# Wider weight transfers in a mixture-of-experts block, and a different hand-over between the engines in its attention and router

## What is computed

```python
proj = rms_norm(x, w) @ w_in                                   # dq, dk, dv, lq, lk, lv
o_diff = rms_norm((softmax(s1) - lam * softmax(s2)) @ dv, subln_w) * (1 - lam_init)
o_dil = (exp(s) * mult / sum(exp(s) * mult)) @ lv              # mult: how many of 3 dilations hold the pair
x1 = x + concat(o_diff, o_dil) @ w_out
h = rms_norm(x1, ffn_norm_w)
logits = h @ router_w + router_b                               # top 4 of 32, gates = softmax of the 4
for e in range(32):                                            # rows of the tokens that chose e
    gu = h[rows] @ w_gate_up[e] + b_gate_up[e]                 # 1024 x 2048: 8 MiB
    y[rows] += gate * ((up + 1) * gate_act @ w_down[e] + b_down[e])   # 1024 x 1024: 4 MiB
out = rms_norm(x1 + y, final_norm_w)
```

## Time and profile before

| | us |
|---|---|
| median of 3 executions (1070.84 to 1072.6) | 1071.29 |
| the profiled execution, its time | 1070.58 |
| its span, first to last instruction | 1068.8 |
| PE busy | 1017.1 (95%) |
| DVE busy | 228.8 (21%) |
| ACT busy | 119.1 (11%) |
| POOL busy | 9.4 (1%) |
| DMA, mean over the span | 397 GB/s |

### The profile page before, as it was taken

One profiled execution on the slowest core, in us unless ns is written; L12 is line 12 of the kernel. 1 busy time (PEld: TensorE's weight loads), 2 busy tenths in 40 slices (PEclk: granted clock), 3 DMA queues, 4 the chain that ended last, 5 costly groups with the idle time before them and its releaser, 6 DMA issues.

```text
span 1068.8 us, 12195 instructions
## 1 busy us (share of the span) xinstructions
PE 1017.1 (95%) x4977; PEld 436.6 (41%) x4977; DVE 228.8 (21%) x511; ACT 119.1 (11%) x287; POOL 9.4 (1%) x23
## 2 busy tenths in 40 slices
PE   9999999999999999999999989898998989898996
PEld 8686544434343434343433324242433333242422
DVE  4476443111111111111111101121211111111111
ACT  1133420000000000000000000000000000000001
POOL 1000000000000000000000000000000000000000
PEclk9999999999999999999999999999999999999999
DMA  9936569999999999999999999999999999999996
GB/s 327 389 129 241 187 248 394 426 428 429 426 429 427 425 430 426 427 429 426 427 430 426 429 430 426 429 430 426 429 429 426 430 429 426 430 428 427 430 423 261
DMA packets 37261, 423.90 MB, mean 397 GB/s; under 512 B 6176, under 2 KB 6192, under 8 KB 12048
## 3 DMA queue, kind: packets, MB, share of 16 engines
q1 hardware_dynamic: 35184, 422.80, 94.2%
q10 hardware_dynamic: 2048, 0.67, 0.2%
HBM read 422.41 MB, written 1.05 MB: 396 GB/s over the span
## 4 chain that ended last, share of the span: by engine, by line
PE 58%; DMA 32%; DVE 6%; SPq 2%; issue 1%; ACT 1%; POOL 0%; DVEq 0%
DMA gu_ring<-in_w_gate_up_dram 32%; PE psum L927 21%; PE psum L977 15%; PE psum L889 5%; PE psum L658 5%; PE psum L633 3%; PE psum L663 2%; PE psum L763 2%; DVE mixed L1386 1%; DVE mixed L1382 1%; DVE mixed L1384 1%; SPq L268 1%; PE psum L705 0%; PE psum L913 0%; ACT mixed L573 0%
## 5 line engine op out<-in xcount | busy, mean ns | idle before, releaser
L927 PE MATMUL psum<-gu_ring,mixed 128*64 128x512 f32 x2048 | 453.4, 595 | 33.9 <-DMA gu_ring<-in_w_gate_up_dram 33.9
L927 PEld LDWEIGHTS psum<-gu_ring,mixed 128*64 128x64 f32 x2048 | 140.9, 137 | 324.4 <-issue 252.7
L977 PE MATMUL psum<-dn_ring,mixed 128*64 128x512 f32 x928 | 206.2, 596 | 3.2 <-ACT mixed L573 2.6
L977 PEld LDWEIGHTS psum<-dn_ring,mixed 128*64 128x64 f32 x928 | 64.9, 137 | 127.5 <-issue 121.9
L1382 DVE TENSOR_SCALAR mixed<-psum 128x512 f32<-128x512 f32 x32 | 22.1, 692 | 425.7 <-PE psum L927 425.7
L1339 DVE TENSOR_TENSOR mixed<-posm,iota 128x256 f32<-128x256 f32 x47 | 20.0, 425 | 243.3 <-PE psum L633 242.9
L591 ACT ACTIVATE mixed<-psum 128x512 f32<-128x512 f32 x30 | 17.9, 597 | 447.9 <-PE psum L927 447.9
L908 PE MATMUL psum<-mixed 64*128 64x512 f32 x256 | 63.6, 615 | 0.7 <-ACT mixed L577 0.7
L889 PE MATMUL psum<-mixed,xres 128*128 128x128 f32 x480 | 59.0, 282 | 0.0
L658 PE MATMUL psum<-gu_ring 128*128 128x256 f32 x256 | 57.5, 382 | 1.1 <-ACT gu_ring L472 1.1
L889 PEld LDWEIGHTS psum<-mixed,xres 128*128 128x128 f32 x480 | 57.9, 197 | 0.0
(11 more groups left out here) (152 smaller groups left out, 386.4 us busy)
## 6 DMA issues: line engine op xcount, KB each, us to landing
gu_ring<-in_w_gate_up_dram SPq DMA_DIRECT2D x123, 2048.0 KB, 28.0
dn_ring<-in_w_down_dram SPq DMA_DIRECT2D x56, 2048.0 KB, 20.1
mixed<-in_w_down_dram SPq DMA_DIRECT2D x6, 2048.0 KB, 13.2
gu_ring<-in_w_in_dram SPq DMA_DIRECT2D x11, 1024.0 KB, 16.1
gu_ring<-in_w_gate_up_dram SPq DMA_DIRECT2D x8, 1024.0 KB, 9.0
dn_ring<-in_w_out_dram SPq DMA_DIRECT2D x4, 1024.0 KB, 9.4
dn_ring<-in_w_down_dram SPq DMA_DIRECT2D x3, 1024.0 KB, 22.4
gu_ring<-in_w_gate_up_dram SPq DMA_DIRECT2D x4, 512.0 KB, 20.9
```

The costliest lines, as they stand in the source:

```text
L927: last = mm(bank[b0 + b][CAP * c:CAP * (c + 1), :], xg[:, k, CAP * half:CAP * (half + 1)], gu_ring[:, 8 * half + k, w0:w0 + 512], start=Fa ...
L977: last = mm(bank[4][CAP * c:CAP * (c + 1), :], actT[:, a0:a0 + CAP], dn_slot[slot][:, k // 2 % 2, w0:w0 + 512], start=False, stop=(k == KT ...
```

## The change

1. **Packets of 32 KB.** Gate/up weights of experts 4 to 31 are laid out with j=4: one chunk then brings each partition four rows, 32 KB side by side. For experts 6 to 29, and the first half of expert 30, a DMA moves such a chunk of 4 MiB (`load_wide`) when two of the former chunks are used; experts 4, 5, the rest of 30 and 31 come in 16 KB (or smaller) parts of those 32 KB. PE waits once in four values of k (`gu_wide`).
2. **x1 turned in place.** To fit j=4 the columns of x1 are rearranged in place before pair 1: ACT copies 512 columns to a PSUM bank, DVE writes them back in the other order, four times, while PE runs `gate_up(1, 0)`; PE waits for the last (`x1_turned`) ahead of pair 1. The gather then reads x1 without a step. The factors of the norm come in a second small load (`ffn_4`).
3. **Dilated heads.** The values are now the stationary operand: `pv_pair` takes two heads, which stand side by side in the array, and gives the result already turned. `pv`, `keep_pv` and `turn_mix` are gone for dilated heads. The division by the sum moves from ACT to POOL (`norm_probs`, two `tensor_scalar` of 256 and 128 columns a head), ahead of the turn. On DVE `dil_probs(g)` stands before `negated_scores(g + 1)` instead of behind it.
4. **Router.** `first_sel` becomes two `tensor_scalar` of 128x64 (compare, then multiply) from `slot0` and `iota_1`; the step L1292 goes behind the first gather; `first_sel(0)` moves ahead of `choose_experts(1)`; the negation for the exponent (L1279) goes behind `chosen_ready`.
5. **Early load.** The second half of w_down of expert 0 comes in two DMAs of 1 MiB; the first is issued when the output projection has used 9 pieces, the second at `x1_done` as before.

```diff
+            def load_wide(e, half, q):
+                r = GUN * half + 4 * q
+                sp.dma_start(gu_ring[:, r:r + 4, :].rearrange("p (e j) c -> p e (j c)", e=1),
+                             gu_v4[:, bass.ds(e, 1), q, :]).then_inc(gu_wide[2 * half + q], 16)
...
                 else:
                     sp.wait_ge(scores_done, 2 * NH)
-                    sp.wait_ge(pv_done, 2 * NH)
+                    sp.wait_ge(pv_done, NH)
+                    sp.wait_ge(mixT_done, NH)
...
             sp.wait_ge(w_out_used, 8)
             load_dn(0, 0, 0)
+            sp.wait_ge(w_out_used, 9)
+            sp.dma_start(dn_ring[:, 2, :], dn_v[:, 0, 1, 0:WS]).then_inc(dn_in[1], 16)
             sp.wait_ge(x1_done, 2 * TT)
-            load_dn(0, 1, 1)
+            sp.dma_start(dn_ring[:, 3, :], dn_v[:, 0, 1, WS:2 * WS]).then_inc(dn_in[1], 16)
...
+            def wide(e, q):
+                sp.wait_ge(gu_used, GUN * (e // 2 - 1) + (4 * (e % 2) + 2 * q + 2) + EXTRA)
+                load_wide(e, e % 2, q)
...
+            def norm_probs(g):
+                pool.wait_ge(sums_ready, g - NH + 1)
+                z = 40 + 2 * (g % 2)
+                for c, w, a in ((0, T, 1), (T, P, 0)):
+                    pr = probs[g % 2][:, c:c + w]
+                    last = nc.gpsimd.tensor_scalar(pr, pr, st[:, z + a:z + a + 1], None, ALU.mult)
+                last.then_inc(probs_ready, 1)
...
+            for i in range(2 * TT):
+                if i:
+                    act.wait_ge(x1_turned, i)
+                nc.scalar.activation(bank[7][:, :], xres[:, i // 2, 512 * (i % 2):512 * (i % 2 + 1)], ACT.Copy)\
+                    .then_inc(x1_copied, 1)
...
+            def pv_pair(g):
+
+                if g == NH:
+                    pe.wait_ge(v_ready, 2)
+                    pe.wait_ge(pv_read, NH)
+                pe.wait_ge(probsT_ready, g + 2)
+                pe.wait_ge(mixT_ready, g // 2)
+                for b in range(2):
+                    for m in range(2):
+                        last = mm(bank[7][HD * m:HD * (m + 1), P + P * b:P + T], vS[:, b, HD * (g + m):HD * (g + m + 1)],
+                                  probsT[m][:, T * b:T + P * b], start=(b == 0), stop=(b == 1), skip_group_check=True)
+                last.then_inc(mixT_done, 1)
...
-                if g + 1 < 2 * NH:
+                if g < NH:
                     negated_scores(g + 1)
-                if g < NH:
                     diff_probs(g)
                 else:
                     dil_probs(g)
+                    if g + 1 < 2 * NH:
+                        negated_scores(g + 1)
...
             def first_sel(a):
-                link(V.tensor_tensor(sel[:, a, :, :], posm[:, a, 2:4].unsqueeze(2).broadcast_to([P, 2, CAP]),
-                                     iota[:, :].unsqueeze(1).broadcast_to([P, 2, CAP]), ALU.is_equal))
-                flat = sel[:, a, :, :].rearrange("p e n -> p (e n)")
-                return V.tensor_scalar(flat, flat, st[:, 2 + a:3 + a], None, ALU.mult)
+                for e in range(2):
+                    last = V.tensor_scalar(sel[:, a, e, :], iota_1, slot0[:, a, e:e + 1], st[:, 2 + a:3 + a],
+                                           ALU.is_equal, ALU.mult)
+                return last
...
+            for i in range(2 * TT):
+                dve.wait_ge(x1_copied, i + 1)
+                V.tensor_copy(xres[:, i // 2, 512 * (i % 2):512 * (i % 2 + 1)].rearrange("t (j p) -> t j p", j=4),
+                              bank[7][:, :].rearrange("t (p j) -> t j p", j=4)).then_inc(x1_turned, 1)
```

More of the change, by code:

```diff
@@ L48 @@
 THREE = 5
+WIDE = 3
 EXTRA = 4
@@ L115, in moe_block @@
         logitsT = part(3072, T)
+        iota_1 = part(2848, CAP)
         iota_e = part(2752, NE)
@@ L354, in dn_two, with load_gu_half @@
                 load_dn(e, q, q)
-            gu(10)
-            gu(11, [0])
+            wide(10, 0)
+            wide(10, 1)
+            wide(11, 0)
             dn_two(10, 0)
             dn_two(10, 1)
-            gu(11, [1, 2, 3])
+            wide(11, 1)
             dn_two(11, 0)
             dn_two(11, 1)
[L364 to L367, removed]
+            def load_gu_half(j, e, half):
+                for q in range(2):
+                    sp.wait_ge(gu_used, j * GUN + (4 * half + 2 * q + 2 - GUN + EXTRA))
+                    load_wide(e + half, half, q)
             def load_dn_both(j, e, half):
@@ L725, in turn_probs @@
                     pe.wait_ge(probsT_ready, g)
-                for b in range(3):
-                    last = turn(bank[6][:, P * b:P * (b + 1)], probs[g % 2][:, P * b:P * (b + 1)])
+                for b, c in enumerate((0, 1, 2) if g < NH else (1, 2, 0)):
+                    last = turn(bank[6][:, P * c:P * (c + 1)], probs[g % 2][:, P * b:P * (b + 1)])
                 last.then_inc(probsT_done, 1)
@@ L880, in first_gather, with gather @@
                 last.then_inc(gather_done, 1)
-            def gather(v):
+            def gather(v, turned=True):
                 pe.wait_ge(sel_ready, v)
@@ L946, in parts_more, with gate_up @@
                 return {0: 32, 1: 16, 2: 16}.get(s, 0)
-            def gate_up(j, half, tail=False, ks=range(KT), b0=2):
+            def gate_up(j, half, tail=False, ks=range(KT), b0=2, wide=True, last_but_one=False):
                 for k in ks:
@@ L998, in turn_act, with expert @@
                 last.then_inc(actT_done, 1)
-            def expert(j, half, loaded, last_one=False):
+            def expert(j, half, loaded, last_one=False, turned=True):
                 def nth(m, c):
@@ L1012, in expert @@
                 else:
-                    gather(j + 2)
+                    gather(j + 2, turned)
                 pe.wait_ge(actT_ready, nth(1, 1))
@@ L1032, in _ @@
             gate_up_bias(2, 1, b0=5)
-            gate_up(0, 1, ks=range(4), b0=5)
+            gate_up(0, 1, ks=range(4), b0=5, wide=False)
             turn_act(1)
-            gate_up(0, 1, ks=range(4, KT), b0=5)
+            gate_up(0, 1, ks=range(4, KT), b0=5, wide=False)
             down_bias(0)
@@ L1056, in _ @@
                 gate_up(j + 1, 0)
+            j = more * PAIRS + (PAIRS - 2)
+            expert(j, 0, loop_down(j, 0))
+            gate_up(j, 1)
+            expert(j, 1, loop_down(j, 1))
+            gate_up(j + 1, 0, last_but_one=True)
             j = more * PAIRS + (PAIRS - 1)
```

162 lines of the change are left out of this document (92 added, 70 removed).

## The result

| | median | of the kernel before |
|---|---|---|
| before | 1071.29 us (1070.84 to 1072.6) | |
| changed | 1078.13 us (1077.5 to 1078.72) | 1.0064, interval 1.0050 to 1.0077 |
| forecast | 1063.6 us (1061.0 to 1068.5) | |

The changed kernel is 6.8 us slower, not 7.7 us faster, and the time lies between the range and rival C. The profiled execution took 1078.72 us, with a span of 1077.0.

A forecast was written before the change was run, and what follows sets the result against it. Memory, streaming expert weights at 428 GB/s, was taken as the bound. An earlier start (3.5 us: router 1.2, heads 2.3) plus packets (4.2) gave 7.7 us less: median 1063.6 us, range 1061.0 to 1068.5.

The forecast's parts named there:

- rival C: Expert loads: rows of twice the pitch are read worse, wide loads lose 2.4%, 11.5 us added, 1079.3 us; chance 0.11.
- the extra small load: ACT in the heads, before the values are kept: one more issue of some 0.5 us, PE waiting later anyway.
- Bounds and rate: Expert loop: memory bounds it at 428 GB/s; 49 wide DMAs save 77 ns each, 4.2 us taken, rate over 431.
- Rivals A and C: A, expert loads: 32 KB rows move like 16 KB ones or are cut; only the start gained, 1067.8 us; chance 0.11.
- Granularity costs nothing: Expert loop: waiting for 4 MiB frees the ring 3.5 us later, but 5.2 us slack a pair and the queue cover it.
- x1 turned: Beside `gate_up(1, 0)`: four copy rounds below 6.4 us fit inside its 14.0 us and cost nothing.
- Router: From the first selection to the first gather: shorter and moved steps gain 1.2 us, ends 0.9 and 1.4.
- Heads: Dilated heads: 3.1 us off PE, less a 0.8 us wait for POOL at the last turn, gain 2.3 us.
- rival B: Dilated heads: POOL or the serial chain on DVE and ACT bounds them, their gain is gone, 1065.9 us; chance 0.12.
- Start of the stream: Expert 2's loads: router and heads together make the weight stream start 3.5 us earlier, ends 2.3 and 4.3.
- part 5: Early 1 MiB down load: takes 2.45 us out of the stretch before expert 2; without it only the heads' gain remains.
- Tail: Behind the last gate/up weights: 24.1 us of the span, taken as unchanged.

The follow-up runs named there:

- e5: Kernel before plus a third small load on ACT, cut to one row of 32 bytes; 1071.21 us, single run.
- e6: Kernel before plus the third small load (256 rows) on ACT, issued ahead of the two others; 1081.06 us, single run.
- e12: Changed kernel with the third small load still on ACT, but issued behind the last head; 1067.44 us, 0.9961 of before.
- e1: Changed kernel with the third small load issued by SP behind expert 1's seventh 2 MiB load, not by ACT; 1067.45 us, 0.9964 of before.
- e3: Kernel before with only the wide packets and turned x1, the small load on SP; 1069.26 us, 0.9982 of before.
- e7: e1 without the pair written out behind PE's loop, expert 30 wholly in wide loads; 1067.11 us, 0.9963 of before.
- e10: Kernel before, 16 KB rows, with PE waiting for two 2 MiB loads at once and SP's loop issuing two together; 1074.88 us, 1.0024 of before.
- e11: e1 without the early half of expert 0's second down load; 1067.1 us, single run.
- e9: e1 with POOL's normalising step cut to one column, which changes the tokens chosen; 2003.7 us, only times up to the first gather read.
- e2: Kernel before plus only the third small load on ACT, its values unused; 1080.53 us, 1.0089 of before.
- e8: Kernel before with the pair before the last written out behind PE's loop; 1072.41 us, 1.0012 of before.
- e4: Kernel before with only the dilated heads, the router and the early half of a down load; 1069.28 us, 0.9986 of before.

## Why the prediction was wrong

**The step that failed** is one sentence of part 2: the extra small load as "one more issue on ACT of some 0.5 us". It measured 8.17 us, and taken away it gives 10.7. I had a row for such an issue (0.4 to 0.6 us) and took its duration as a property of the instruction. But the issue stands when too many rows are in ACT's queue (e5, e6, e12), and at this place it held 1536 that hardly moved, because SP's two loads of 2 MiB had gone out just before. I said that PE "waits later anyway" behind it; in fact the next work on ACT, keeping the values, was what PE needed next, with 0.5 us to spare, as the code's `v_ready` and the rows of ACT and PE at 112.8 and 113.3 us would have told me. Nor was this among my rivals: each of them was about a resource that the change meant to use, none about its smallest line. With the load elsewhere the kernel takes 1067.4 us, inside the range, though 3.8 above the forecast: the range held for what I had counted, but several terms of the sum were off. That rest goes as follows, e1 against before, in their profiles.

- **Bounds and rate**: right. The memory bounds the loop, a wide DMA saves 80 ns (forecast 77), the rate rose to 430 or 431 (I had asked for over 431). Rivals A and C fell.
- **"Granularity costs nothing"**: wrong. I looked only at whether the queue holds, and it does. I did not look at the end, where PE works off the last two pairs. Before, PE had 3.5 us of matmuls left at a landing, now 7.0, and in the changed kernel, e3, e7, e10 and e11 no DMA stands in the chain of the last 80 us. The longer waits also cost clock, 1.7 us for each row of 3.4 us (8.81 us for 32 matmuls instead of 7.11). Inside the loop that is hidden by the next wait; ahead of the last two pairs it is not (below). e10's profile prices it at 2.5 us at the end. In e1 and e12 it was masked: their weights landed late, and a DMA is in the chain to 1041 us.
- **The written-out pair**: not in my sum at all. Two more fetches of code, which delayed the last weights by 1.5 us in e1 and e3. For e1's last landing the pieces close: 0.7 us from the start of the stream, 49 x 0.08 = 3.9 from the packets, 1.5 lost here, which makes the 3.1 us.
- **x1 turned**: right. In e1 its four rounds run from 215.7 to 221.1 us, inside `gate_up(1, 0)` (215.5 to 229.4), and PE doesn't wait for them. What I left out is a small gain: the gather's 32 matmuls take 3.57 us without the step, 3.77 with it.
- **Router**: forecast 1.2, measured 1.0: from PE's turn ahead of it to the gather 169.78 - 166.44 = 3.34 us against 160.30 - 156.03 = 4.27 (the turn's start in the chain of before), and 0.05 less idle time on the way.
- **Heads**: forecast 2.3, measured 1.0 from the last differential `pv` to the turn of x1 behind the heads (109.60 to 144.88 us, in e1 109.89 to 144.16); 0.7 in absolute time. `pv_pair` was 0.80, near the 0.77 taken. What was off is the sum: a pair of heads fell from 6.6 to 6.1 us, where I had 5.74. Two out-projections took 1.81 instead of 1.72, and the turns of two heads 0.80, where I had counted 0.68 (0.77 in the kernel before). A removed turn of a pair was worth 0.27 from start to start, not 0.37. PE also waited 1.22 instead of 0.66 us for ACT's copy ahead of the first pair. POOL's step was 1.5 us where I took 1.0; e9 shows what it costs, 1.06. Inside a pair PE has no wait, so rival B, a chain through DVE, ACT and POOL that bounds the heads, is not what took the rest.
- **Start of the stream**: forecast 3.5 us earlier, measured 1.7 for the first gate/up (160.69 against 162.38). For the landings from 188 us on it is 0.7 in e1 and 1.1, 1.4 and 2.8 in e9, e12 and e7, which have the same code up to there: one profile is not enough to size this term. That part 5 was needed for it is not borne out (e11).
- **Tail**: 24.1 forecast, 23.9 measured.

The changed kernel's chain ahead of its last two pairs:

```profile
959.86 34.63 DMA gu_ring<-in_w_gate_up_dram
...
994.53 8.81 PE psum L983 x32
...
1017.88 13.76 PE psum L983 x64
...
1042.89 13.91 PE psum L983 x64
```

Busy time by stretch around its start (after ACT and POOL: granted clock, DMA share, GB/s):

```profile
988.00:994.40 6.40, 3.90 (x20) 1.01 (x16) 0.00 (x0) 0.00 (x0) 0.00 (x0) 1.00 0.93 397
994.60:998.00 3.40, 3.40 (x10) 0.96 (x12) 0.00 (x0) 0.00 (x0) 0.00 (x0) 0.50 1.03 439
```

PE had been idle for 2.63 us before 994.53, at the upper level of 2.4 GHz, and then worked 3.4 us at the lower of 1.2 GHz. The weights landed at 1054.61, and PE ended them at 1056.8, 2.2 us later instead of 1.1. This, or the row of half clock that the changed kernel's profile has at 8.2 us and e1's has not, may be why e1's edit took away 10.7 us and e2's added only 9.5; the intervals overlap, so it isn't shown.

The Trainium skill's rule that I weighed ("SBUF — State Buffer", Who interferes with whom) cost nothing here: DVE's probabilities (L1250 in e1) take 0.42 to 0.43 us as before, since POOL worked beside the negated scores. At one place it may show, small: POOL's last step ran beside a DVE product of two SBUF inputs (L1307) and took 1.60 us instead of 1.50. A DVE copy and other short steps ran beside it too, so which of them cost the 0.1 us isn't told apart.

Open: why the first 3.4 us of half clock stand at 8.2 us in the changed kernel's profile and in those of e8, e9 and e10, and not in before's or e1's. It costs about 1.7 us in such an execution. As kernels with and without each part show it, I take it for no effect of the change; that is argued, not shown, and it can blur a difference of 2 us between two profiles. Nor was a kernel tried that has wide rows, no written-out pair and fine waits at once.

## What to carry to other kernels

The price of a DMA issue is not that of the instruction alone: count the rows already in the engine's queue and ask what large loads stand beside them, and put many small rows on an engine that nobody waits for, or where its queue is empty. When waits become coarser, ask not only whether the queue holds but how much work is left behind the last landing, and what the longer idle time does to the clock. An edit's smallest line deserves the question "who is queued behind it" as much as its largest.

## What the runs showed of the hardware

- A DMA issue on ACT stood for 8.06 to 8.30 us with 1792 rows in small DMAs and two 2 MiB loads of SP in flight; with 1537 rows it took 0.40 (e5), and with 256 rows alone 0.41 (e12). It ended when 1689 to 1696 packets were left, in three kernels.
- Beside rows of 16 KB, small rows moved about one for one (147 to 131 in 5 us); without them, 1211 in a microsecond.
- Rows of 32 KB took 1.21 to 1.22 us, of 16 KB 0.61 to 0.62; a wide DMA of 4 MiB saves 80 ns over two of 2 MiB.
- A code fetch of 16 KB took 1.0 to 1.1 us of one DMA engine and lengthened the 32 KB row behind it from 1.22 to 1.71 us. It delayed the load beside it by 1.5 us (e1, e3), 1.2 (changed), 1.0 (e12), 0.4 (e8, e11) or not at all (e1's fetch at 970.0).
- PE's granted clock fell to half for 3.4 us in the loops whose longest wait for weights was 2.6 or 2.7 us (changed, e1, e3, e7, e10, e11, e12), though not behind each such wait, and never in those where it was 1.2 or 1.3 us (before, e2, e4, e5, e6, e8).
- A multiplication by a scalar per partition takes POOL 0.94 us for 128x256 and 0.60 us for 128x128.
